# Two weight-block sums of the down product made in DRAM by accumulating DMAs

## The reference

```python
p = rms_norm(h_res) @ w_cat                      # 2048 -> 6432 columns
y_conv = short_conv_group(p[..., :N_CONV_COLS])  # gated convolution, width 3
y_rwkv = rwkv7_group(token_shift(p[..., N_CONV_COLS:]))  # 16 heads of 64: a recurrence over tokens
h_res = h_res + concatenate([y_conv, y_rwkv]) @ w_out
h = rms_norm(h_res)
h_res = h_res + square(relu(h @ w_up)) @ w_down  # 2048 -> 8192 -> 2048
out = rms_norm(h_res)[:, N_META:]
```

## Time and profile before

| | |
|---|---|
| median of 3 runs | 2352.21 us (2349.92 to 2354.92) |
| the profiled execution | 2349.79 us, its span 2348.1 us |
| granted PE clock | 0.998 of full speed |
| PE | 2320.8 us, 99% |
| PE weight load | 2087.0 us, 89% |
| DVE | 1491.3 us, 64% |
| ACT | 1019.9 us, 43% |
| POOL | 299.7 us, 13% |
| queue q1 | 224.19 MB, 34.6% of the 16 engines' span |
| queue q0 | 56.20 MB, 11.8% |

### The profile page before, as it was taken

How to read it: one execution, slowest core, us unless ns; L and a number is a source line. 1 busy time by engine, 2 the same in 40 slices (tenths; PEclk the granted TensorE clock), 3 DMA queues, 4 the chain that set the end, 5 groups by cost and what they waited for, 6 DMA issues and landing times.

```text
span 2348.1 us, 49773 instructions
## 1 busy us (share of the span) xinstructions
PE 2320.8 (99%) x18736; PEld 2087.0 (89%) x18736; DVE 1491.3 (64%) x2338; ACT 1019.9 (43%) x1808; POOL 299.7 (13%) x340
## 2 busy tenths in 40 slices
PE   8999999999999999999999999999999999999998
PEld 8999999999999788889889889889889899899888
DVE  7558668568567654548558468467467476475356
ACT  6534434434344322435435345345345344354336
POOL 5102011011012132101001001001001001001007
PEclk9999999999999999999999999999999999999999
DMA  8244243343343643526527527537447347347434
GB/s 253 72 108 101 68 112 80 93 103 75 98 103 100 181 130 98 179 86 144 145 72 160 138 81 162 131 94 168 110 98 177 99 101 175 94 117 195 120 110 142
DMA packets 513298, 286.18 MB, mean 122 GB/s; under 512 B 84510, under 2 KB 490528, under 8 KB 512672
## 3 DMA queue, kind: packets, MB, share of 16 engines
q1 hardware_dynamic: 478512, 224.19, 34.6%
q0 software_dynamic: 24064, 56.20, 11.8%
q10 hardware_dynamic: 10496, 2.62, 0.6%
HBM read 232.47 MB, written 50.47 MB: 121 GB/s over the span
## 4 chain that ended last, share of the span: by engine, by line
PE 91%; DVE 3%; DMA 3%; issue 1%; ACT 1%; SPq 0%; ACTq 0%; DVEq 0%
PE PD L1894 42%; PE PD L1899 18%; PE PW L2167 5%; PE PW L2168 5%; PE PW L2169 5%; PE PD L2167 2%; PE PD L2168 2%; PE PD L2169 2%; PE PD L2113 1%; PE PD L1923 1%; PE PW L1923 1%; DMA w_raw<-in_w_in 1%; PE PW L1973 1%; DMA gram<-NA 1%; PE PW L2073 1%
## 5 line engine op out<-in xcount | busy, mean ns | idle before, releaser
L1894 PE MATMUL PD<-act_lo,w_hi 128*128 128x512 f32 x1344 | 531.6, 396 | 0.0
L1894 PE MATMUL PD<-act_hi,w_hi 128*128 128x512 f32 x1344 | 529.5, 394 | 0.5 <-issue 0.5
L1894 PE MATMUL PD<-act_hi,w_lo 128*128 128x512 f32 x1344 | 528.5, 393 | 0.0
L2167 PE MATMUL PW<-form_hi,w_hi 128*128 128x256 f32 x1120 | 313.4, 280 | 0.0
L2169 PE MATMUL PW<-form_hi,w_lo 128*128 128x256 f32 x1120 | 312.6, 279 | 0.0
L2168 PE MATMUL PW<-form_lo,w_hi 128*128 128x256 f32 x1120 | 312.6, 279 | 0.0
L1894 PEld LDWEIGHTS PD<-act_hi,w_hi 128*128 128x128 f32 x1344 | 252.4, 188 | 62.7 <-issue 2.0
L1894 PEld LDWEIGHTS PD<-act_hi,w_lo 128*128 128x128 f32 x1344 | 252.9, 188 | 57.5
L1894 PEld LDWEIGHTS PD<-act_lo,w_hi 128*128 128x128 f32 x1344 | 252.1, 188 | 57.8 <-issue 0.2
L1345 DVE TENSOR_TENSOR w_lo<-w_raw,w_hi 128x512 fp32r<-128x512 f32 x268 | 206.7, 794 | 109.0 <-ACT w_hi L930 105.7
L930 ACT CAST w_hi<-w_raw 128x512 fp32r<-128x512 f32 x268 | 160.4, 620 | 252.2 <-DMA w_raw<-in_w_in 113.6
(11 more groups left out here) (378 smaller groups left out, 4080.7 us busy)
## 6 DMA issues: line engine op xcount, KB each, us to landing
w_raw<-in_w_in SPq DMA_DIRECT2D x200, 256.0 KB, 3.2
w_raw<-in_w_down SPq DMA_DIRECT2D x136, 256.0 KB, 3.0
w_more<-in_w_down SPq DMA_DIRECT2D x136, 256.0 KB, 3.1
w_raw<-in_w_up SPq DMA_DIRECT2D x128, 256.0 KB, 3.1
w_more<-in_w_up SPq DMA_DIRECT2D x128, 256.0 KB, 3.4
residual<-delta POOLq DMA_DIRECT2D x56, 512.0 KB, 5.8
w_raw<-in_w_out SPq DMA_DIRECT2D x64, 256.0 KB, 2.8
residual<-res POOLq DMA_DIRECT2D x4, 2048.0 KB, 10.1
```

Of the source, the lines that this page charges most:

```text
L1894: ins = M(pd_seq(n)[:, 0:width], w, v[:, k, first:first + width], start=begin, stop=end)
L2167: M(bank_for(product, p), whi, hi, start=begins and k == 0, stop=False, skip_group_check=True)
```

## The change

For every group g of the seven, two of the sums are made in DRAM. `second_row_sum[g]` and `first_column_sum[g]` are new tensors of 512 x 1024 (2 MB). POOL copies the block a21 of `w_down` into each (`copy_block`, 512 rows of 4 KB, DRAM to DRAM), and, when the copy has landed, adds a22 or a11 with an accumulating DMA (`add_block`). For groups 0 to 3 this lies in the mixing stage, one copy and one add in each of the 8 pairs: the copy at the head of POOL's part of the pair, the add between `rb_lo` and the masks. For groups 4 to 6 both copies and both adds stand at the head of POOL's part of MLP groups 0 to 2. SP loads five quarters for each p instead of four: a11, s1, a12, a22 and s3, where s1 and s3 come from the new tensors. DVE keeps two sums of 128 x 512 for each p. L_GROUP becomes 72 loads.

```diff
-BLOCKS = ("a11", "a21", "a22", "a12")
-BLOCK_IN = {"p1": "a11", "p2": "a12", "p4": "a22"}
+BLOCKS = ("a11", "s1", "a12", "a22", "s3")
+BLOCK_IN = {"p1": "a11", "p5": "s1", "p2": "a12", "p4": "a22", "p7": "s3"}
+NB = len(BLOCKS)
+FREED_BY = (3, 3, 4, 5, 7)
+SUM_IN = {"p6": 0, "p3": 1}
+SUMMED_IN_MIX = 4
...
+        def copy_block(g, column):
+
+            dst = s3_dram if column else s1_dram
+            pool.dma_start(dst[g], wdn_halves[g, 1, 0]).then_inc(block_copied[column], 16)
+
+        def add_block(g, column, copies, per=0, it=0):
+
+            pool.wait_ge(block_copied[column], at(16 * copies, 16 * per, it))
+            pool.sem_inc(copy_seen, 1)
+            dst = s3_dram if column else s1_dram
+            pool.dma_start(dst[g], wdn_halves[g, 1 - column, 1 - column], accum_op=ALU.add).then_inc(block_summed, 16)
...
+            copy_block(j // 2, j % 2)
             if not last:
                 pool.wait_ge(pe_done, step(PE_STEPS, "low", j))
                 load_wa(j + 1)
...
             done("rbl", nc.gpsimd.tensor_tensor(rb_lo, ld[:, 0:SEQ], rb_hi.bitcast(F32), ALU.subtract))
+            add_block(j // 2, j % 2, j // 2 + 1)
             pool.wait_ge(dve_done, step(DVE_STEPS, "gram0", j))
...
+        with pool.Fori(0, FFG - 1 - SUMMED_IN_MIX) as g:
+            copy_block(g + SUMMED_IN_MIX, 0)
+            add_block(g + SUMMED_IN_MIX, 0, SUMMED_IN_MIX + 1, 1, g)
+            copy_block(g + SUMMED_IN_MIX, 1)
+            add_block(g + SUMMED_IN_MIX, 1, SUMMED_IN_MIX + 1, 1, g)
+            add_deltas(g)
...
-            if product in ("p1", "p5"):
-                sum_blocks(p, 1 if product == "p1" else 2, it)
+            if product in ("p5", "p2"):
+                sum_blocks(p, 0 if product == "p5" else 1, it)
...
-                V.tensor_tensor(flat(w_sum[:, 0:2]), flat(raw[:, 1:2]).to_broadcast([P, 2, KQ * P]), flat(raw[:, 0:3:2]),
-                                ALU.add).then_inc(sum_made, 1)
...
+                V.tensor_tensor(w_sum[:, 0], raw_mlp(at_), raw_mlp(at_ + 1), ALU.add).then_inc(sum_made, 1)
```

More of the change, by code:

```diff
@@ L217 @@
 R_GROUP = R_UP + NP * HALF_KT
-L_GROUP = 4 * UT + 4 * HALF_KT
+L_GROUP = 4 * UT + NB * HALF_KT
 R_LAST = Q_MLP + R_GROUP * (FFG - 1)
@@ L512, in hybrid_layer @@
     wdn_q = w_down.rearrange("(g a k p) (m n) -> g a p k m n", g=FFG, k=KQ, p=P, n=P)
+    wdn_halves = w_down.rearrange("(g y r) (x n) -> g x y r n", g=FFG, y=2, x=2)
+    sums_q = [d.rearrange("g (k p) (m n) -> g p k m n", p=P, n=P) for d in (s1_dram, s3_dram)]
     RS_CUT = META + 3 * P
@@ L620, in _ @@
                 for b, name in enumerate(BLOCKS):
-                    rel = R_UP + 4 * p + b
-                    load_mlp(wdn_q[g, int(name[2]) - 1, :, :, p + HALF_KT * (int(name[1]) - 1), :], rel, freed_by(rel - RAW_MLP), g)
+                    rel = R_UP + NB * p + b
+                    if name[0] == "s":
+                        if p == 0:
+                            sp.wait_ge(block_summed, at(32, 32, g))
+                            sp.sem_inc(sum_seen, 1)
+                        src = sums_q[name == "s3"][g, :, :, p, :]
+                    else:
+                        src = wdn_q[g, int(name[2]) - 1, :, :, p + HALF_KT * (int(name[1]) - 1), :]
+                    load_mlp(src, rel, freed_by(rel - RAW_MLP), g)
             for t in range(RAW_MLP // 4):
@@ L838, in _, with add_deltas @@
             pool.wait_ge(delta_added[h], 16)
-        with pool.Fori(0, FFG - 1) as g:
+        def add_deltas(g):
             for p in range(HALF_KT):
@@ L845, in _ @@
                                accum_op=ALU.add).then_inc(delta_added[p % 2], 16)
+        with pool.Fori(0, FFG - 1 - SUMMED_IN_MIX) as g:
[4 more added lines that the diff above has]
+            add_deltas(g)
+        with pool.Fori(FFG - 1 - SUMMED_IN_MIX, FFG - 1) as g:
+            add_deltas(g)
         for parity in range(2):
@@ L1310, in split_mlp @@
             V.tensor_tensor(w_lo[:, r], src, w_hi[:, r].bitcast(F32), ALU.subtract).then_inc(lo_split, 1)
-            if product in ("p1", "p5"):
-                sum_blocks(p, 1 if product == "p1" else 2, it)
+            if product in ("p5", "p2"):
+                sum_blocks(p, 0 if product == "p5" else 1, it)
         def sum_blocks(p, which, it):
[L1316 to L1320, removed]
+            at_ = R_UP + NB * p
             if which == 0:
-                for name in ("a11", "a21", "a22"):
-                    loaded(name)
+                dve.wait_ge(hi_split, at(Q_MLP + R_UP + NP * p + 2, R_GROUP, it))
                 dve.wait_ge(lo_split, at(Q_MLP + R_UP + NP * p, R_GROUP, it))
-                flat = lambda ap: ap.rearrange("p s k n -> p s (k n)")
-                V.tensor_tensor(flat(w_sum[:, 0:2]), flat(raw[:, 1:2]).to_broadcast([P, 2, KQ * P]), flat(raw[:, 0:3:2]),
-                                ALU.add).then_inc(sum_made, 1)
[L1329 to L1335, removed]
+                V.tensor_tensor(w_sum[:, 0], raw_mlp(at_), raw_mlp(at_ + 1), ALU.add).then_inc(sum_made, 1)
+            else:
+                dve.wait_ge(hi_split, at(Q_MLP + R_UP + NP * p + 3, R_GROUP, it))
+                dve.wait_ge(sum_made, at(2 * p + 1, 2 * HALF_KT, it))
+                V.tensor_tensor(w_sum[:, 1], raw_mlp(at_ + 2), w_sum[:, 0], ALU.add).then_inc(sum_made, 1)
         def split_last(i):
```

22 lines of the change are left out of this document (10 added, 12 removed).

## The result

The change takes 2440.06 us, median of 4 runs (2435.65 to 2443.21), against 2353.57 of before (4 runs, 2349.92 to 2355.51): a ratio of 1.0368, 95% interval 1.035 to 1.0386. The forecast was 2438. The profiled execution took 2435.65 us, its span is 2434.1, which is 86.0 more than the 2348.1 of before.

The account below looks back on a forecast made before the run. The prediction took PE's own work as the bound, busy 2320.8 of 2348.1 us. Its terms, -6.1 for DVE's sums and +94.9 for the pairs' adds, the rest 0, gave +88.8 on 2349.8: 2438 us, range 2364 to 2478.

Parts of the forecast that it names:

- Part 1: MLP, behind tile 7: without the wide and one narrow sum the forms start earlier, all seven PE waits go: -6.1 us.
- Part 2: Down half: 56 more loads of 256 KB, covered by the two rings: 0 us.
- Part 3: MLP groups 0 to 2: two copies and two adds in a row, covered by the rings and gaps: 0 us.
- its step about loads that land in the gaps: MLP up half: of 19 quarters in the transfer stretch, 16 are in the rings and about 12 can land in three gaps.
- Part 4: Mixing stage: each pair's 2 MB copy keeps engines busy 6.5 us and ends before the cast needs its weight load: 0 us.
- Part 5: Mixing stage: each pair's add, 14.5 us of all engines, makes `gram<-NA` and the exchange land 12.6 us late: +94.9 us.
- a queue that came first is emptied before the other gets a turn: DMA engines in each pair: `gram<-NA` moves nothing until the add's data end at 675.9, landing 12.6 us late.
- the rule of turns that the prediction set aside: Trainium skill: each DMA engine goes round its queues, draining a packet of typically 9 to 17 descriptors before switching; total 2370.
- DVE waits about 14 us a pair: Sign of being right: DVE waits about 14 us in each pair for `UU<-gram`, instead of 1.8.
- shared turns: Rival, exchange beside the add: q0 and q1 split the engines evenly, 3.7 us late a pair, 2370 us; chance 0.09.
- The fast add: Rival, add in each pair: takes 6.5 us like a plain transfer, exchange 4.6 us late, 2375 us; chance 0.08.
- No collision: Rival, mixing stage: the add is clear of the exchange or small transfers go first; only 6.1 us gained, 2343.7; chance 0.08.

Follow-up runs that it names:

- the last kernel: The change with no copy or add in the mixing stage, group 0's in the output product, each MLP group making the next's, spaced: 2338.61 us, 0.9954 of before.

## Why the prediction was right

- **Part 1, DVE's sums**: the direction and the place were right, the size was not: 10 us in the MLP (10.0 by the spans, 14.3 by the medians of the whole) for 6.1. The term summed brackets of idle time, and these are short where matmuls overlap and where the restart itself is slow. DVE's busy time fell by 46.8 us instead of 68. 14 of the 21 missing are the `w_lo` of the mixing and output stages, 848 ns for 794 on the mean of 268, by the splits of 4.0 us. In the run without transfers it fell by 55.2, so some are still unaccounted for.
- **Part 2, the fifth load**: 0, confirmed by the run without copies and adds.
- **Part 3, the MLP's transfers**: wrong, 8 us for 0. The text's own sign for it, a wait for `w_lo`, is there, but its step about loads that land in the gaps is not what failed. The chain took 56 us, from 1074.9 to 1130.8 in the first group, close to the 53 that 19 quarters of 2.8 us make, and in that group PE never waits, though the second copy ran into the first add (issued 0.7 us behind it, landed after 24 us). The text counted only weight loads as what the transfers could hold up. PE's two waits are beside the first copy of groups 1 and 2, where the loads are in time and the program's code is late.
- **Part 4, the copy in each pair**: right. It takes 6.5 us of the engines, as summed, and lands after 9.9, and no wait of PE answers to it.
- **Part 5, the add in each pair**: 92 us for 94.9, and 12.2 us late for 12.6. Two of its steps were off and offset each other. The add needs 11.5 us of the engines, not 14.5, so its rate is better than a delta's (the upper bound of 20 rested on no row). And "a queue that came first is emptied before the other gets a turn" is wrong: the turns go packet by packet, nearer to the rule of turns that the prediction set aside, and q1's small packets get little out of it, but some. With the time that q1 takes and a slower start the add lands 17.5 us after its issue, so its end stands nearly where the forecast of 14.5 had put it, and `gram<-NA` lands 2 us behind that. The 2.9 us by which `gram<-NA` is issued later were not foreseen, and cost nothing. "DVE waits about 14 us a pair" was 92.0 / 8 = 11.5.
- The place of PE's wait was wrong: not `x16`, but the projection 9 us earlier, whose PSUM bank waits for DVE's `cu`. DVE's order puts `cu` behind its wait for the exchange. I had followed the chain to the engine at its end and not asked what else stands behind DVE's wait.
- Not in the sum at all: the granted clock. Of the 86 us 16.5 are longer busy time of PE, nearly all of it at the lower clock after its waits. In the mean of seven pairs PE waits 9.3 us ((54.0 + 10.8) / 7), and from one pair's `gram<-NA` to the next it is 102.4 us for 90.8, 11.6 more, so some 2 us of it are the clock. On the other side PE's wait was shorter than the exchange's delay, which the forecast had put at the same size. That sum and forecast agree to 2 us is partly luck in these terms: the MLP's 8 us, part of the gain of DVE's sums and the clock were all missing from it.
- The rivals: shared turns at even halves (2370) fell. The turns are shared in packets, not in time. The fast add of 6.5 us (2375) fell by the measured 11.5. No collision (2343.7) fell for this place, and the last kernel shows what it asked for: free of the exchange and away from the head of an MLP group, the work costs 3 us or nothing.

## What to carry to other kernels

Before a large DMA is called hidden, look for the small transfers that will be under way beside it, and follow who waits for them: 11.5 us of engine time cost next to nothing beside weight loads that are issued eight quarters ahead (some 22 us, at 2.8 a quarter), and 12 us a pair beside an exchange with 0.4 in hand. The program's own code is loaded beside them on the DMA engines, so the head of a loop may be such a place too. Follow a late transfer to every engine that waits for it, and to what is queued behind that wait, for the first to run dry may be reached by a side way, as `cu` here. And if a large transfer has to run, put it where only loads with depth are beside it, away from its like and from the head of a loop: the same bytes gave +86 us in one place and -11 in another.

## What the runs showed of the hardware that was not expected

- Two queues with work on the same DMA engines took turns about packet for packet (421 to 347 with 0.5 KB against 4 KB; 285 to 297 with the 64 bytes of `UU<-gram` against 4 KB, from 741 to 747 in the run with the add behind the masks), with no regard for size: with packets of 0.5 KB the small queue moved 0.21 MB in 8 us. The stretch that had misled the forecast is the first 4.7 us of such a backlog, 25 packets to 430; in the next 3.5 us of the same trace it is 290 to 290. The other traces have such a start too: 9 to 165 packets from 736 to 741 with the add behind the masks, though `UU<-gram` is issued at 736.29. What holds q1 back at first stays open.
- 2 MB accumulated from DRAM into DRAM took 11.5 us of all engines in rows of 4 KB and 13.6 in rows of 1 KB; the plain copy took 6.5.
- SP itself stood in the issue of `gram<-NA`: up to 8.1 us for one instruction, where it took 0.6 to 0.7 with the add of one row. Everything behind it on SP waits as long. In the run with the add behind the masks it is the weight load behind `UU<-gram` that takes 7.85. What SP waits for inside the issue is not shown.
- A wait of 8.6 us was followed by 2 us at a granted clock of 0.50 and 2 us at 0.62, and one of 2.25 us by 3.4 us at 0.52, with the matmuls at nearly half their rate. PE's wait costs its length and this.
- 16 KB of code that started 2.2 us late or more at the head of an MLP group, behind a copy of 2 MB, stood in front of a wait of PE of 2.25 us or more each time; the profile puts such a wait down to "issue" or to a `w_lo` that was nearly or long done.
